# Differences of summed decays by a constant stationary triangle and 512-column moving operands in two parts

## What is computed

```python
G = jnp.cumsum(g, axis=-1)
decay = jnp.exp(jnp.where(causal, G[..., :, None] - G[..., None, :], -jnp.inf))
lower = jnp.where(strict, jnp.einsum('bhnid,bhnjd->bhnij', k_beta, k) * decay, 0.0)
intra = jnp.where(causal, jnp.einsum('bhnid,bhnjd->bhnij', q, k) * decay, 0.0)
```

## Time and profile before

| what | value |
|---|---|
| median of 3 runs | 1353.49 us (1353.31 to 1355.42) |
| profiled execution, its own time | 1355.88 us |
| its span, first to last instruction | 1354.10 us |
| PE busy | 1329.6 us, 98% of the span |
| DVE busy | 756.1 us, 56% |
| ACT busy | 479.3 us, 35% |
| POOL busy | 181.2 us, 13% |
| mean granted clock of PE | 0.998 |

### The profile page before, as it was taken

One profiled execution on the slowest core, in us unless ns is written; L12 is line 12 of the kernel. 1 busy time (PEld: TensorE's weight loads), 2 busy tenths in 40 slices (PEclk: granted clock), 3 DMA queues, 4 the chain that ended last, 5 costly groups with the idle time before them and its releaser, 6 DMA issues.

```text
span 1354.1 us, 24412 instructions
## 1 busy us (share of the span) xinstructions
PE 1329.6 (98%) x10477; PEld 1116.6 (82%) x10477; DVE 756.1 (56%) x1287; ACT 479.3 (35%) x787; POOL 181.2 (13%) x132
## 2 busy tenths in 40 slices
PE   9899999999999999999999999999989999999997
PEld 8689888877888888888878888888988888888786
DVE  6885237844766756777545634555366522355335
ACT  5354433443524434435335321113453222222220
POOL 1102000030000220001200142233212200022000
PEclk9999999999999999999999999999999999999999
DMA  6064312222122222122222366653333233233311
GB/s 222 27 225 129 109 63 101 78 71 80 48 87 101 79 80 72 55 72 100 88 72 78 126 215 211 190 163 132 138 94 110 94 124 94 93 94 93 109 63 62
DMA packets 59458, 143.66 MB, mean 106 GB/s; under 512 B 5032, under 2 KB 23896, under 8 KB 59352
## 3 DMA queue, kind: packets, MB, share of 16 engines
q1 hardware_dynamic: 59352, 142.12, 32.2%
HBM read 127.40 MB, written 16.27 MB: 106 GB/s over the span
## 4 chain that ended last, share of the span: by engine, by line
PE 90%; DVE 6%; ACT 1%; issue 1%; DMA 1%; SPq 0%; DVEq 0%; ACTq 0%
PE acc L1842 18%; PE acc L1844 17%; PE acc L1843 17%; PE ps_a L1844 2%; PE ps_a L1842 2%; PE ps_a L1843 2%; PE ps_d L2028 2%; PE ps_a L1951 2%; PE ps_d L2161 2%; PE ps_a L2161 2%; PE ps_d L2163 2%; PE ps_a L2163 2%; PE ps_d L2162 2%; PE ps_a L2162 2%; PE ps_a L1962 1%
## 5 line engine op out<-in xcount | busy, mean ns | idle before, releaser
L1367 DVE TENSOR_TENSOR w_lo<-w_raw,w_hi 128x1024 fp32r<-128x1024 f32 x172 | 230.6, 1342 | 213.6 <-ACT w_hi L1047 213.1
L1842 PE MATMUL acc<-n_hi,w_hi 128*128 128x512 f32 (+1 forms) x776 | 313.0, 403 | 3.5 <-ACT conv_x L1122 3.0
L1047 ACT CAST w_hi<-w_raw 128x1024 fp32r<-128x1024 f32 x172 | 180.2, 1049 | 384.6 <-PE acc L1844 315.0
L1844 PE MATMUL acc<-n_hi,w_lo 128*128 128x512 f32 (+1 forms) x776 | 300.6, 387 | 0.0
L1843 PE MATMUL acc<-n_lo,w_hi 128*128 128x512 f32 (+1 forms) x776 | 299.8, 386 | 0.0
L1842 PEld LDWEIGHTS acc<-n_hi,w_hi 128*128 128x128 f32 x776 | 146.4, 189 | 33.7 <-issue 6.1
L1844 PEld LDWEIGHTS acc<-n_hi,w_lo 128*128 128x128 f32 x776 | 146.1, 188 | 30.6
L1843 PEld LDWEIGHTS acc<-n_lo,w_hi 128*128 128x128 f32 x776 | 146.7, 189 | 25.1
L1004 POOL TENSOR_SCALAR gate_st<-gate_st 128x512 f32<-128x512 f32 x24 | 23.9, 996 | 461.9 <-ACT gate_st L1129 461.9
L1842 PE MATMUL acc<-y_hi,w_hi 128*128 128x512 f32 x192 | 74.7, 389 | 0.0
L1843 PE MATMUL acc<-y_lo,w_hi 128*128 128x512 f32 x192 | 74.7, 389 | 0.0
(11 more groups left out here) (404 smaller groups left out, 2501.2 us busy)
## 6 DMA issues: line engine op xcount, KB each, us to landing
w_raw<-weights SPq DMA_DIRECT2D x200, 512.0 KB, 3.5
gate_scratch<-gate_st SPq DMA_DIRECT2D x24, 256.0 KB, 2.2
g_in<-gate_scratch SPq DMA_DIRECT2D x24, 256.0 KB, 3.9
y_raw<-y_scratch SPq DMA_DIRECT2D x16, 256.0 KB, 3.8
x_tok<-x SPq DMA_DIRECT2D x4, 512.0 KB, 5.1
y_scratch<-y_st SPq DMA_DIRECT2D x4, 512.0 KB, 3.1
y_scratch<-d_ET SPq DMA_DIRECT2D x4, 512.0 KB, 4.1
y_scratch<-y_st SPq DMA_DIRECT2D x8, 256.0 KB, 2.4
```

The source lines that it names most:

```text
L1047: nc.scalar.copy(hi_of_tile(t), w_raw[:, t % RAW]).then_inc(hi_ready, 1)
L1367: V_.tensor_tensor(lo_of_tile(t), w_raw[:, t % RAW], hi_of_tile(t).bitcast(F32), ALU.subtract).then_inc(lo_ready, 1)
L1842: mm(bank, wh, hi_of(k), start=start and k == 0, stop=False)
L1844: last = mm(bank, wl, hi_of(k), start=False, stop=stop and k == KT - 1)
```

## The change

`dE` is turned round. The triangle A, a constant, is the stationary operand (`after_r`, type fp32r, written once), and the triangle U times the decays is the moving operand, four chunks or 512 columns at a time. As one fp32r number would not hold a decay, the decays are split once into a high and a low part (`g_parts`, 32 columns each, over parameters that have been used by then), POOL multiplies U by both in each pair (`sums_hi`, `sums_lo`), and PE adds the two products in the same bank: four products of 128x512 in the place of eight of 128x128 in fp32. The new tiles share their place with `d_ET` and `d_AT`. The constants are loaded by two DMAs in the place of one, with one block of 128x128 left out. Two numbers of the planner's tables change: `dE` on PE from 1.79 to 0.91, `dk` on POOL from 2.0 to 4.8.

```diff
-PE_US = {"dE": 1.79, ...
+PE_US = {"dE": 0.91, ...
-POOL_US = {"dk": 2.0, "dkT": 2.0, "dkb": 2.0, "dL": 2.5, "dA": 4.5}
+POOL_US = {"dk": 4.8, "dkT": 2.0, "dkb": 2.0, "dL": 2.5, "dA": 4.5}
...
+        after_r = sb("after_r", [P, P], F32R)
...
-        U, SCR, K, KB, V, TF, QT, KTT, KBT, ET, LT, AT, TT = (B[n] for n in names)
+        U, SCR, K, KB, V, TF, QT, KTT, KBT, LT, TT = (B[n] for n in names)
+        c1 = ExitStack()
+        sc_ = sb_in(c1)
+        ET, AT = sc_("d_ET", [P, 8, P]), sc_("d_AT", [P, 8, P])
+        c1.close()
+        sums_hi, sums_lo = sd_("sums_hi", [P, 8, P], F32R), sd_("sums_lo", [P, 8, P], F32R)
...
-            sp.dma_start(cst[:, C_ID + 1:], consts[:, C_ID + 1:]).then_inc(in_cst, 16)
+            sp.dma_start(cst[:, C_ID + 1:S_EYES], consts[:, C_ID + 1:S_EYES]).then_inc(in_cst, 16)
+            sp.dma_start(cst[:, S_CAUS], consts[:, C_CAUS]).then_inc(in_cst, 16)
...
-                    last = nc.gpsimd.tensor_tensor(ET[:], over(cst[:, C_AFTER, :], 8),
-                                                   along(flat(gdec[:, heads]), P), ALU.mult)
+                    g_hi, g_lo = (g_parts[:, n, 8 * p:8 * p + 8] for n in range(2))
+                    nc.gpsimd.tensor_tensor(sums_hi[:], over(cst[:, C_UPTO, :], 8), along(g_hi, P), ALU.mult)
+                    last = nc.gpsimd.tensor_tensor(sums_lo[:], over(cst[:, C_UPTO, :], 8), along(g_lo, P), ALU.mult)
...
-                V_.scalar_tensor_tensor(out=gdec[:], in0=ba[:, 1], scalar=-1.0, in1=along(ealog, ST),
-                                        op0=ALU.mult, op1=ALU.mult).then_inc(g_ready, 1)
+                link(V_.scalar_tensor_tensor(out=gdec[:], in0=ba[:, 1], scalar=-1.0, in1=along(ealog, ST),
+                                             op0=ALU.mult, op1=ALU.mult))
+                V_.tensor_copy(after_r[:], cst[:, C_AFTER, :])
+                link(V_.tensor_copy(g_parts[:, 0].bitcast(F32R), flat(gdec[:])))
+                V_.tensor_tensor(g_parts[:, 1], flat(gdec[:]), g_parts[:, 0], ALU.subtract).then_inc(g_ready, 1)
...
                 elif kind == "dE":
-                    for m in range(8):
-                        last = mm(dst[m], ET[:, m], cst[:, C_UPTO, :], start=True, stop=True)
+                    for n in range(2):
+                        for part in (sums_hi, sums_lo):
+                            last = mm(ps_d[:, n], after_r[:], part[:, 4 * n:4 * n + 4].rearrange("p a b -> p (a b)"),
+                                      start=part is sums_hi, stop=part is sums_lo)
```

More of the change, by code:

```diff
@@ L56 @@
 NCONST = 4 + NM
+S_EYES, S_CAUS = 8, 9
 PC_PRE, PC_MEM, PC_FF = 0, 8, 16
@@ L72 @@
          "dU": "A", "dW": "A", "sa": "D", "sb": "AD", "dO": "D"}
-PE_US = {"dE": 1.79, "dL": 1.79, "dA": 1.79, "dU": 1.79, "dW": 1.79, "T1": 0.55, "Za": 0.55, "Wb": 1.05, "Z5": 0.55, "W5": 0.9, "Zl": 1.2, "Wl": 1.2, "sa": 0.45,
+PE_US = {"dE": 0.91, "dL": 1.79, "dA": 1.79, "dU": 1.79, "dW": 1.79, "T1": 0.55, "Za": 0.55, "Wb": 1.05, "Z5": 0.55, "W5": 0.9, "Zl": 1.2, "Wl": 1.2, "sa": 0.45,
          "sb": 1.35, "cs": 3.44, "cv": 3.43, "as0": 1.3, "as1": 1.35, "at": 1.09, "ap": 2.24, "av": 0.44, "ay": 0.44}
@@ L458, in build @@
         w_lo = sb("w_lo", [P, SPL, KT, P], F32R)
-        cst = sb("cst", [P, NCONST, P])
+        cst = sb("cst", [P, S_CAUS + 1, P])
+        after_r = sb("after_r", [P, P], F32R)
         ones = sb("ones", [P, P])
@@ L497, in build @@
         sd_ = sb_in(dl)
-        names = ["U", "SCR", "K", "KB", "V", "TF", "QT", "KTT", "KBT", "ET", "LT", "AT", "TT"]
+        names = ["U", "SCR", "K", "KB", "V", "TF", "QT", "KTT", "KBT", "LT", "TT"]
         B = {n: sd_("d_" + n, [P, 8, P]) for n in names}
-        U, SCR, K, KB, V, TF, QT, KTT, KBT, ET, LT, AT, TT = (B[n] for n in names)
+        U, SCR, K, KB, V, TF, QT, KTT, KBT, LT, TT = (B[n] for n in names)
[4 more added lines that the diff above has]
+        sums_hi, sums_lo = sd_("sums_hi", [P, 8, P], F32R), sd_("sums_lo", [P, 8, P], F32R)
         WT, O = SCR, LT
@@ L512, in build @@
         Y, Y5, Y6 = part_of(KTT, 0), part_of(KTT, 1), part_of(KTT, 2, P // 2)
-        eyes = cst[:, C_MASK0 + NM - 1, 0:QB]
+        eyes = cst[:, S_EYES, 0:QB]
         c1 = ExitStack()
@@ L692, in build @@
         block = ctx.enter_context(nc.Block())
+        g_parts = par[:, PC_LAM:PC_LAM + 2 * HB * ST].rearrange("p (a b) -> p a b", a=2)
         LAMS, LAME, NLAM = smd[:, 2:4], smd[:, 4:6], smd[:, 6:7]
@@ L1443, in beta_and_decay @@
                 link(V_.tensor_scalar(NLAM, NLAM, LAM_INIT, None, ALU.subtract))
-                dve.wait_ge(in_cst, 16)
+                dve.wait_ge(in_cst, 32)
                 for q in range(1, 4):
@@ L1514, in attn @@
                         link(V_.tensor_tensor(strip[:, :, P:2 * P], strip[:, :, P:2 * P],
-                                              over(cst[:, C_CAUS, :], HA), ALU.add))
+                                              over(cst[:, S_CAUS, :], HA), ALU.add))
                     ps = flat(ps_a[:])
@@ L2046, in decay @@
                 pe.wait_ge(g_ready, 1)
-                pe.wait_ge(in_cst, 16)
+                pe.wait_ge(in_cst, 32)
                 pe.wait_ge(ones_set, 1)
```

## The result

| | before | changed |
|---|---|---|
| median of 4 runs each | 1354.45 us | 1361.57 us |
| lowest and highest | 1353.31, 1357.03 | 1360.14, 1362.82 |
| ratio, with its 95% interval | | 1.0051 (1.0039 to 1.0063) |
| profiled execution, its own time | 1355.88 us | 1360.89 us |
| mean granted clock of PE | 0.998 | 0.994 |

The change makes the kernel slower by 0.51%, some 7 us. The prediction, 1355.0 us in a range of 1350.6 to 1357.4, was wrong: it held "no difference" for the likeliest, and the time lies 4.2 us over its range. About 1 us of that is the starting point: the kernel before stood at 1353.5 us in the three runs that the prediction went from, and at 1354.5 with a fourth.

A forecast was written before the change was run, and what follows sets the result against it. PE bounds the kernel (98% busy), with DVE setting its pace until 91 us. Terms -3.4 + 0.55 + 1.7 + 0.5 + 0.5 = -0.15, plus 1.6 for the clock, about +1.5 on 1353.5: 1355.0 us, range 1350.6 to 1357.4.

The forecast's parts named there:

- no difference: Whole kernel: time between 1350.8 and 1356.2 us, within 0.2% of the kernel before; chance 0.62.
- `dE` on PE: PE's `dE` step in four pairs: four products replace eight, sparing 0.85 us each, -3.4 us.
- The decays: Start of DVE's chain before 91 us: cast and subtraction release PE later, once, +0.55 us.
- The second multiply: First pair, POOL beside DVE's convolutions: DVE loses time again and the queries come later, +1.70 us.
- The clock at 90 us: PE before the first pair's queries: a 3.1 us wait likely drops the clock to 1.2 GHz, +1.6 us.
- The third and fourth `dkT`: PE's `dkT` in pairs three and four: waits for DVE's `d_KB`, about +0.5 us each.
- The sum of the instructions: Whole kernel: all terms together, -0.15 us with the clock held, about +1.5 us if it falls at 90 us.
- a held clock: Rival at the first pair's queries: the clock does not fall, sum -0.15 us, 1353.3 us; chance 0.25.
- the new lists bring more starved bursts: Rival, fourth pair's 32x32 bursts: another 1.5 us "issue" wait, sum +3.0, 1356.5 us; chance 0.18 shared with another case.
- another case: Rival at `dE`: a 512-column product takes 0.45 us, saving nothing, sum +3.3 to +4.9; shares the 0.18.

The follow-up runs named there:

- 0.9991 to 0.9967: Kernel before with POOL's first-pair multiply held back until the queries are done, 0.9991; the change on the old list with decays on POOL and multiplies held back, 0.9967.
- the change on the old list: Changed kernel with the planner's `dE` number put back to 1.79, so engines follow the kernel before's instruction order: 1356.76 us, ratio 0.9998.
- the old instructions on the new list: Kernel before with only the planner's `dE` number set to 0.91, giving the changed kernel's instruction order: ratio 1.0043.
- 16 main parts: Changed kernel with the planner's DVE maximum moved from 3.6 to 4.68, so branch A's last step stands 16 main parts before the mixing: ratio 1.0027.
- The eight tiles: Changed kernel, PE's and ACT's order untouched, with each of the eight reloads of attention outputs given its own tile: ratio 1.0019.

## Why the prediction was wrong

Point by point, in the order of its sum:

- *`dE` on PE*, -3.4: right. 0.23 us a product in all four pairs, 3.3 us by starts, and 3.3 us in the time once DVE is out of the way (0.9991 to 0.9967).
- *The decays*, +0.55: right, 0.59 from `gdec` to PE.
- *The second multiply*, +1.70: right in kind; 1.5 us in the experiment that adds it alone. In the changed kernel the multiplies took 1.90 to 2.88 us each, the longest above the 1.9 to 2.4 that the prediction gave.
- *The clock at 90 us*, +1.6: 1.5 us where it happens, but it doesn't always. Behind a wait of 2.1 us it fell in three of the profiled executions and held in four. The term should have been a chance of about a half, not a certainty.
- *The third and fourth `dkT`*, +0.5 each: right in kind, half the size, 0.25 and 0.29 us by starts. On the old list the third pair's is 0.24 us (`d_KB` ends at 460.49, `dkT` starts at 460.63), and the fourth pair's step is held up no more.
- *The sum of the instructions*, -0.15 or, with the clock, +1.5: the change on the old list measured -1.5 to +0.9. The sum with a held clock lies in that, the one that was forecast lies 0.6 us above it. With the sizes read from the changed kernel's trace and 1.5 for the multiply it is -3.26 + 0.59 + 1.5 + 0.25 + 0.29 = -0.6 us, and +0.9 where the clock falls.
- *The failed step* is the rival "the new lists bring more starved bursts". Apart from the fourth pair's 0.5 us, it was the only place in which the moved list had a price; the sum itself had the rest of the list at nothing. The price was taken from the one kind of list-made wait that the trace of before showed, "issue", and it was put at +1.5 us, with a chance of 0.18 together with another case. In fact those waits all but went away in the changed kernel (with the old instructions on the new list 2.6 us of them stayed), and the list cost 5.8 us at a place that I did not look at. The difference of the lists that I did quote, branch B's fourth pair, was harmless. The one that decided was at the end of the list: branch A's last step went from 29 to 15 main parts before the mixing. The trace of before had what was needed to see it: the last store at 763.5 us, the last `y_lo` done at 800.4 and PE's arrival at 804.9, so 4.5 us of slack for a chain that was going to start 14 main parts, or 19 us, later. That gives the sign, not the size: by it the last `y_lo` would be done 14.6 us after PE's arrival, and it was done 10.0 us after (812.8 for 802.85), since the chain from the store on took 29.5 us where it had taken 36.9.

The planner does not know this either. In its model the reloads are steps that nothing on PE waits for, so a list that ends branch A late looks as good to it as one that ends it early. A single number of the tables moved by 15 or 30% leaves the step where it is in more than half of the cases, and else puts it anywhere from 14 to 33 main parts before the mixing. So a true number put in the place of a false one can hurt as well as help.

What stays open: why the clock falls behind one wait of 2.1 us and not behind another; how the 5.8 us of the list divide in the executions without a profile, since the profiled one shows 8.7; and why 16 main parts cost so much less than 15. The eight tiles took the waits for `y_lo` away and put another in their place, so no run has the changed kernel's own list without either; that the chain cost 7.0 us in its profiled execution rests on the starts of the products.

## What to carry to other kernels

When an edit changes a scheduler's table, split it into two kernels, the new instructions on the old order and the old instructions on the new order, before anything is said of either; here that took one number each, and the two parts came out as 0.0% and +0.43%. To price a moved order from the old trace, look at the end of each branch's list: find the chain from its last step through store, reload and split to the first consumer, and set its length against the distance to that consumer; read the result as a warning, since its size came out too large here. Look for delays in the distances of starts too, because a list of waits can hide those shorter than a record's overlap. And a wide POOL operation belongs where DVE doesn't set the pace, even if its result is ready only just in time.

## What the runs showed of the hardware

The length of a wait alone doesn't say whether the clock falls behind it. Behind the same wait of 1.52 to 1.55 us at about 56.7 us it fell to 1.2 GHz in four of the 14 profiled executions, the kernel before among them, and held in ten. In those ten PE then waited 2.8 to 3.4 us for the decays, and the clock fell behind that wait each time; in the other four that wait was only 1.2 to 1.8 us, and the clock fell behind it in two. Behind 2.1 us before the queries it fell in three of seven, as said. In the changed kernel it was the wait for the decays, 3.38 us:

```profile
64.60 0.77 PE L1855 MATMUL acc<-n_hi,w_hi 128*128 128x512 f32 x1
...
69.44 0.46 PE L1857 MATMUL acc<-n_hi,w_lo 128*128 128x512 f32 x1
```

Between these two starts lie eleven distances, 4.84 us, which at 0.227 take 2.50. That is 2.3 us of PE and nothing of the time: DVE sets the pace there, and PE's waits of 1.45 us (before, for `conv_x` at 67.64) and 0.79 us (before, for `d_V` at 75.04) are gone in exchange. Later on the clock costs time only in a stretch where PE itself is the bound, as behind the queries and behind the reloads at 813 us.

POOL's multiply takes 1.90 us when it is not held up, and up to 2.96 us beside DVE, and not because of its fp32r output: in fp32, done twice in the kernel before, it took 1.99 and then 2.34 us in the first pair. What the longer ones contain can be read in the third pair of the changed kernel, POOL and then DVE:

```profile
448.31 1.90 POOL L989 TENSOR_TENSOR sums_hi<-cst,par 128x1024 fp32r<-128x1024 f32 x1 [38.62 <-PE ps_d L1998]
450.17 2.88 POOL L990 TENSOR_TENSOR sums_lo<-cst,par 128x1024 fp32r<-128x1024 f32 x1
...
448.52 2.77 DVE L1377 TENSOR_TENSOR w_lo<-w_raw,w_hi 128x1024 fp32r<-128x1024 f32 x1 [3.56 <-ACT w_hi L1057]
451.21 2.92 DVE L1571 TENSOR_TENSOR d_SCR<-d_K 128x1024 f32<-128x1024 f32 x1
```

The ends alternate: POOL at 450.21, DVE at 451.29, POOL at 453.05, DVE at 454.13. From the other engine's end to its own, DVE's split takes 1.08 us and its square 1.08 (1.22 each when undisturbed), and POOL's second multiply 1.76. So here the two engines work in turns, an instruction at a time, as in the exclusive lock for a whole instruction that the prediction cites from the Trainium skill (SBUF — State Buffer, "SBUF: two separate sides"). In the first pair DVE lost 3.2 us (7.91 for 4.68) to two multiplies that take 3.8 us when they are not held up, 0.3 us less apiece than the full length; the 4.62 us that they took there are longer by POOL's own waiting.
